# Three expert-row tiles a head turned ahead of the sweep, in halves over three buffer pairs, and zero writes moved behind the norm roots

## What is computed

```python
h = _rms(x, attn_norm_g[l])
proj = h @ w_in[l]                       # q, k, v (1024 each), then cb, cc, cx of the short convolution
q = _rms(q...); k = _rms(k...)           # per head norms, 8 heads
a = _diff_attention(q, k, v, lam)        # two softmaxes a head, their weighted difference, times v
a = (_rms(a, subln_g[l]) * (1.0 - lam_init)).reshape(b, s, ATTN_WIDTH)
c = _short_conv(cb, cc, cx, conv_w[l])
x = x + jnp.concatenate([a, c], axis=-1) @ w_out[l]
x = x + _peer(_rms(x, ffn_norm_g[l]), peer_w_q[l], peer_subkeys[l], peer_u[l], peer_v[l])
```

## Time and profile before

| what | value |
| --- | --- |
| median of 3 runs | 2966.29 us |
| the profiled execution | 2965.18 us, of which the span is 2963.4 us |
| PE, DVE, ACT, POOL busy | 98%, 80%, 35%, 51% of the span |
| granted TensorE clock | 0.995 over the span, 1.00 in the stretches shown below |
| HBM | 866.33 MB read, 112.33 MB written |

### The profile page before, as it was taken

The page is one execution under the profiler, slowest core; times in us unless marked ns, Lnnn a source line. Parts: engine busy times, 40 slices in busy tenths (PEclk is TensorE's granted clock), DMA queues, the critical chain, the costliest instruction groups (busy, mean ns, idle before and its releaser), DMA issues.

```text
span 2963.4 us, 40377 instructions
## 1 busy us (share of the span) xinstructions
PE 2892.9 (98%) x14993; PEld 2571.4 (87%) x14993; DVE 2356.5 (80%) x3050; ACT 1049.3 (35%) x1373; POOL 1510.2 (51%) x906
## 2 busy tenths in 40 slices
PE   8999999999999999999999999999999999999998
PEld 6888777888889999999999999999997788777777
DVE  6455677755688888988888898899777999998898
ACT  4122343341323333434333343334233333333333
POOL 1000232300016666665665666566867778877852
PEclk9999999999999999999999999999999999999999
DMA  8998777779658998999999899999999999999998
GB/s 297 332 348 278 253 237 252 226 289 332 225 187 305 320 340 302 337 320 330 309 322 337 305 339 316 333 343 356 338 348 395 412 415 410 417 418 419 419 417 357
DMA packets 324223, 980.65 MB, mean 331 GB/s; under 512 B 62756, under 2 KB 179504, under 8 KB 240752
## 3 DMA queue, kind: packets, MB, share of 16 engines
q1 hardware_dynamic: 179488, 508.60, 46.5%
q0 software_dynamic: 107008, 439.75, 41.3%
q10 hardware_dynamic: 37584, 30.43, 3.2%
HBM read 866.33 MB, written 112.33 MB: 330 GB/s over the span
## 4 chain that ended last, share of the span: by engine, by line
PE 66%; DVE 15%; DMA 10%; issue 4%; ACT 3%; POOL 1%; ACTq 0%; DVEq 0%; SPq 0%; POOLq 0%
PE ps L1827 21%; PE ps L1829 20%; PE ps L1828 20%; DMA v_two<-in_peer_v 9%; DVE x_rows L1685 3%; PE ps L2079 3%; DVE u_row L1676 2%; DVE v_lo L1725 2%; ACT v_hi L1196 2%; DVE x_one L1775 1%; DMA v_ring<-in_peer_v,experts 1%; DVE uT_lo L1670 1%; DVE uT_lo L1665 1%; PE ps L1910 1%; PE ps L1926 1%
## 5 line engine op out<-in xcount | busy, mean ns | idle before, releaser
L1827 PE MATMUL ps<-hT_hi,uT_hi 128*128 128x384 f32 x2048 | 699.0, 341 | 10.5 <-DVE uT_lo L1665 8.6
L1829 PE MATMUL ps<-h2T_lo,uT_hi 128*128 128x384 f32 x2048 | 686.1, 335 | 0.0
L1828 PE MATMUL ps<-hT_hi,uT_lo 128*128 128x384 f32 x2048 | 684.9, 334 | 0.0
L831 POOL DMA_INDIRECT gate_grid<-gates,grid_cells x256 | 541.5, 2115 | 107.4 <-issue 78.8
L1827 PE MATMUL ps<-v_hi,a_hi 128*128 128x512 f32 x1024 | 405.7, 396 | 31.5 <-DVE v_lo L1725 30.7
L1828 PE MATMUL ps<-v_hi,a_lo 128*128 128x512 f32 x1024 | 402.5, 393 | 0.0
L1829 PE MATMUL ps<-v_lo,a_hi 128*128 128x512 f32 x1024 | 402.3, 393 | 0.0
L1827 PEld LDWEIGHTS ps<-hT_hi,uT_hi 128*128 128x128 f32 x2048 | 384.7, 188 | 19.4 <-DVE uT_lo L1665 14.6
L1196 ACT ACTIVATE v_hi<-v_two 128x2048 fp32r<-128x2048 f32 x126 | 241.3, 1918 | 448.1 <-PE ps L1829 324.9
L1828 PEld LDWEIGHTS ps<-hT_hi,uT_lo 128*128 128x128 f32 x2048 | 385.0, 188 | 1.9
L1829 PEld LDWEIGHTS ps<-h2T_lo,uT_hi 128*128 128x128 f32 x2048 | 384.3, 188 | 0.0
(11 more groups left out here) (209 smaller groups left out, 4975.9 us busy)
## 6 DMA issues: line engine op xcount, KB each, us to landing
v_two<-in_peer_v SPq DMA_DIRECT2D x63, 2048.0 KB, 11.8
u_tile<-in_peer_u SPq DMA_DIRECT2D x72, 1024.0 KB, 8.0
u_tile<-uT_all SPq DMA_DIRECT2D x56, 1024.0 KB, 6.8
near_rows<-in_peer_u SPq DMA_DIRECT2D x40, 1024.0 KB, 8.3
uT_all<-near_turned SPq DMA_DIRECT2D x100, 256.0 KB, 7.0
w_raw<-in_w_in SPq DMA_DIRECT2D x24, 1024.0 KB, 9.3
wc_raw<-in_w_in SPq DMA_DIRECT2D x48, 512.0 KB, 6.6
far_rows<-in_peer_u SPq DMA_DIRECT2D x16, 1024.0 KB, 9.4
```

Source lines behind the costliest of these rows:

```text
L831: pool.indirect_dma_start(out=gate_grid, out_offset=bass.IndirectOffsetOnAxis(ap=grid_cells[:, d, col:col + 1], axis=0), in_=gates[:, 2 + ...
L1827: mm(out, a_hi, b_hi, start=first, stop=False)
L1828: mm(out, a_lo, b_hi, start=False, stop=False)
L1829: return mm(out, a_hi, b_lo, start=False, stop=last)
```

## The change

Seven more tiles, one for each of heads 0 to 6, are turned ahead: tile 6 of groups 0 to 6 of the sweep (`EXTRA_AT`). So three tiles a head are turned, in six halves (1024 of the 2048 columns, 512 KB each). Half i uses buffer pair (third, left, right)[i % 3]: left and right are the halves of the old pair, the third is new. DVE turns half 0 at the head's start, 1 and 2 where the first tile's halves were, 3 behind `combined(3)`, 4 and 5 behind `o_n`. SP loads the halves between the pieces, behind `wc_ready` of pieces 1 to 5. POOL stores each half by four DMAs of 128 KB in runs of 1 KB. The zeros move from the head's start to behind the two roots. Ahead of its loop over the heads SP now waits until the last q, k, v chunk is finished (the third pair lies where weights of that stage are), so pieces 2 and 3 of head 0 are issued behind that. In the sweep both u buffers can hold a turned tile. Some semaphores are merged.

```diff
 def turned_before(tile):
+    if tile % TOPK == EXTRA_AT:
+        return tile // TOPK < EXTRA
+    return tile % 2 == 1 and tile < 2 * ODD_TURNED
-    return tile % 2 == 1 and tile < 2 * TURNED
...
@@ SP @@
+            for t in range(TB):
+                sp.wait_ge(proj_done[t], QKV_CHUNKS)
             with sp.Fori(0, CT - 1) as j:
                 for p in range(PIECES):
                     sp.wait_ge(wc_ready, PIECES * j + p + 1)
                     conv_piece(j + (p + 2) // PIECES, (p + 2) % PIECES)
-                    if p in (2, 5):
-                        next_rows(NEAR, 2 * j + (NEAR_HEADS + p // 5))
+                    for i in ((), (0,), (1, 2), (3,), (4,), (5,))[p]:
+                        next_half(j, i)
...
+            sp.wait_ge(half_kept[THIRD], 16 * QUADS * HALF_USES)
             load_mix(MIX_ORDER[1])
@@ POOL @@
+            def store_half(x, row, half):
+                rows = uT_all[bass.ds(row * P, P), :].rearrange("(r d) (a h m) -> a h d r m", r=QUADS, a=QUADS, h=HALVES)
+                for a in range(QUADS):
+                    pool.dma_start(rows[a][half], half_turned[x][QUAD * a:QUAD * (a + 1), :, :, :].rearrange("d r k e -> d r (k e)"))\
+                        .then_inc(half_kept[x], 16)
...
             for j in range(HEADS):
-                for n in range(2 * j, 2 * j + 2):
-                    zero_cells(n)
                 if j > 0:
                     store_o(j - 1)
                 if j < HEADS - 1:
-                    keep_turned(NEAR_HEADS + 1 + 2 * j)
+                    for i in range(4):
+                        keep_half(j, i)
...
                 if j < HEADS - 1:
...
-                    keep_turned(NEAR_HEADS + 2 + 2 * j)
+                for n in range(2 * j, 2 * j + 2):
+                    zero_cells(n)
+                if j < HEADS - 1:
+                    for i in range(4, 6):
+                        keep_half(j, i)
...
@@ DVE @@
+            def turn_half_of_head(j, i):
+                x, use = half_of_head(i), 2 * j + i // 3
+                dve.wait_ge(half_in[x], 16 * (HALF_LOADS[x] + use) + 16)
+                dve.wait_ge(half_kept[x], 16 * QUADS * (HALF_STORES[x] + use))
+                turn_half(x)
...
                 if not last:
+                    turn_half_of_head(j, 3)
                     split_wc(j + 1, 1)
```

More of the change, by code:

```diff
@@ L454, in decoder_layer, with odd, odd_of_head, extra @@
         nc_block = ctx.enter_context(nc.Block())
[L457 to L462, removed]
+        def odd(pair, n):
+            k = n + pair * (NEAR_TURNED - EXTRA)
+            return 2 * k + 1, k
+        def odd_of_head(j, m):
+            k = NEAR_HEADS + 2 * j + m
+            return 2 * k + 1, k
+        def extra(j):
+            return TOPK * j + EXTRA_AT, ODD_TURNED + j
+        def store_turned(engine, pair, row, stored):
+            rows = uT_all[bass.ds(row * P, P), :].rearrange("(r d) (a m) -> a d r m", r=QUADS, a=QUADS)
             for a in range(QUADS):
@@ L465, in store_turned, with half_place, half_of_head, halves_turned @@
                     .then_inc(stored, 16)
+        def half_place(j, i):
+            place = extra(j) if i >= 4 else odd_of_head(j, 1 + i // 2)
+            return place, i % 2
+        def half_of_head(i):
+            return (THIRD, LEFT, RIGHT)[i % 3]
+        def halves_turned(j, i):
+            return 4 * (NEAR_HEADS + 1) + 2 * (6 * j + i)
         @nc_block.sync
@@ L475, in load_quarter, with load_rows, load_half, next_half @@
                     .then_inc(w_in_raw[q % 2], 16)
[L477 to L481, removed]
-                sp.wait_ge(seg_ready[pair], 4 * n + 4)
[L484 to L491, removed]
+            def load_rows(pair, tile):
+                sp.dma_start(seg_rows[pair][:, :], u_table[bass.ds(tile * P, P), :]).then_inc(seg_in[pair], 16)
+            def load_half(x, tile, half):
+                cols = slice(half * D // HALVES, (half + 1) * D // HALVES)
+                sp.dma_start(half_rows[x][:, :], u_table[bass.ds(tile * P, P), cols]).then_inc(half_in[x], 16)
+            def next_half(j, i):
+                (tile, _), half = half_place(j, i)
+                sp.wait_ge(seg_ready[NEAR], halves_turned(j, i) - 4)
+                load_half(half_of_head(i), tile, half)
+            def keep_turned(pair, n, place, then=None):
+                sp.wait_ge(seg_ready[pair], 4 * n + 4)
+                if then is not None:
+                    load_rows(pair, then[0])
+                store_turned(sp, pair, place[1], seg_stored[pair])
             def load_wi(c, q):
@@ L497, in load_qkv_weights, with keep_odd @@
             def load_qkv_weights():
+                def keep_odd(pair, n, last=False):
+                    keep_turned(pair, n, odd(pair, n), None if last else odd(pair, n + 1))
                 def chunk(c, first=False):
@@ L533, in far, with keep_odd @@
                     return FAR_QKV + 2 * c
+                def keep_odd(pair, n, last=False):
+                    seen = EXTRA if pair == NEAR else 0
+                    keep_turned(pair, n, odd(pair, n - seen), None if last else odd(pair, n - seen + 1))
                 for q in range(1, 4):
@@ L1412, in head @@
                                    vec[:, V_CONV:N_VEC].rearrange("p (a c) -> p a c", a=TAPS)[:, :, bass.ds(j, 1)]))
+                if not last:
+                    turn_half_of_head(j, 0)
                 def biased(qb):
@@ L1444, in head @@
                 if not last:
-                    turn_rows(NEAR, 2 * j + (NEAR_HEADS + 1), "heads", range(2))
+                    turn_half_of_head(j, 1)
                 split_wc(j, 4)
@@ L1449, in head @@
                 if not last:
-                    turn_rows(NEAR, 2 * j + (NEAR_HEADS + 1), "heads", range(2, 4))
+                    turn_half_of_head(j, 2)
                 biased(3)
@@ L1474, in head @@
                 if not last:
[L1475 removed]
+                    turn_half_of_head(j, 4)
+                    turn_half_of_head(j, 5)
                     norm_qk(j + 1, 1)
@@ L1519, in rest_of_chunk @@
                 split_wo(c + 1, 1)
-                turn_rows(NEAR, 3 * c + NEAR_OUT, "heads" if first else "out")
+                if first:
+                    for x in (LEFT, RIGHT):
+                        dve.wait_ge(half_kept[x], 16 * QUADS * (HALF_STORES[x] + HALF_USES))
+                turn_rows(NEAR, 3 * c + NEAR_OUT, "out")
             split_wo(0, 3)
```

172 lines of the change are left out of this document (104 added, 68 removed).

## The result

The changed kernel takes **3005.32 us** in the median of 4 runs (3003.94 to 3008.36), the kernel before 2966.32 (2965.81 to 2966.8); the ratio is 1.0137, with a 95% interval of 1.0125 to 1.0149. The forecast was 2962.2, its range 2956 to 2976. The profiled execution of the changed kernel is the one of 3008.36 us, with a span of 3006.6 and a granted clock of 0.985 over the span, where before had 0.995.

The account below looks back on a forecast made before the run. PE was taken to bound the heads and sweep groups 0 to 5, with group 6 nearly DVE's. Steps 1 to 5 summed as -10.5 + 2.2 + 0 + 4.2 + 0 = -4.1 us, giving 2962.2 us, range 2956 to 2976.

Parts of the forecast that it names:

- Step 1: Sweep: PE loses tile 6's transposes, 1.76 us a tile in groups 0 to 5, nothing counted in group 6; -10.5 us.
- Step 2: Start of the heads: SP's new wait delays pieces 2 and 3 of head 0, so PE stands once; +2.2 us.
- Step 3: DVE and POOL work in a head: extra half turns and store issues fit in free time, zeros delay none; 0 us.
- Step 4: DMA engines in a head: extra loads and stores leave transfers over, 0.6 us a head for seven heads; +4.2 us.
- Rival B: Heads: weight pieces starve in DMA queues, half 1 comes late, about 3 us a head; +12.7 us, 2979; chance 0.22.
- The rule weighed: DMA queues: each engine goes round its queues, taking a whole packet from one before changing; alone it would give rival B.
- Step 5: End of the heads: the last zeros, written later, delay following loads by up to 1 us within slack 1.8; 0 us.
- Rival A: Heads: left-over transfers are absorbed behind the sensitive piece, so step 4 is 0; -8.3 us, 2958.0; chance 0.37.
- Rival C: Sweep: DVE already sets the pace about tile 6, so the change doesn't shorten it; 2968 to 2975; chance 0.03.

Follow-up runs that it names:

- the kernel with the well-placed zeros: Changed kernel with a head's two zero DMAs parted, one behind the stores of half 2, one between the two roots: 2958.25 us, ratio 0.9971.
- the fastest kernel: Changed kernel with zero DMAs behind half 2's stores and between the roots, and SP's wait behind the issue of head 0's piece 3: 2953.47 us, ratio 0.9957.

## Why the prediction was wrong

**What bounds the kernel.** Right: PE bounded the heads without a wait, and they could only get longer.

**Step 1, right.** Forecast -10.5 in the sweep and nothing in group 6. From the first product of group 0 to that of group 6 it took 1036.4 us before and 1025.9 after; group 6 took 153.3 and 153.2. The whole time fell by 11.2 us in the run of that part alone. PE makes 1040 transposes instead of 1152.

**Step 2, the mechanism right, the size too small.** Forecast 2.2 us; the gap is 3.0 us (2.8 with that wait alone), inside the bounds of 1.9 to 4.8. What the sum lacked is that the wait costs more than its length: 4.7 us to the start of the sweep.

**Step 3, right as far as it goes.** PE waits for neither `o_ss` nor `qk_ss`, and with the zeros elsewhere DVE's 2.6 us more and POOL's 16 more issues cost nothing (heads of 40.90 us). Its last sentence, that the zeros behind the roots delay none, is true of the roots and says nothing of SP's loads.

**Step 4 is the one that failed.** Its amounts were good: with the zeros well placed the share is 0.93, and I had 0.91 to 0.97. But the sum spread the cost as bytes over free engine time and asked what was left at the end of the busy stretch. From that came 0.6 us a head, where 8.0 were measured. The sum had no term for the order in which POOL's and SP's transfers meet. I counted it as a gain that "the zeros now start just after the empty stretch"; just there SP issues piece 4. Before, that piece and the tile's load were issued 4.3 and 3.6 us ahead of the zeros (419.33 and 420.05 against 423.67). What the runs showed in its place is a wait for transfers that are issued behind the zeros: piece 4 lands 17 us and half 1 18.6 us after its issue, DVE stands for 8.55 us, PE for 5.2, and the slower clock comes on top. The bounds of 0 and 20 for seven heads did not hold the measured 48 either.

**Rival B, right in place and sign, too small in size.** I gave it 0.22 and 3 us a head. It took a piece's 13.0 us, the longest of the earlier trace rows, as the most that sharing could cost; 17 us were measured. But in the kernel before that 13.0 is itself a piece behind zeros. POOL's zeros and SP's next issues in head 3, and the landing of the first of these, piece 5:

```profile
423.67 1.78 POOL L776 DMA_DIRECT2D gate_grid<-zeros  x2
...
424.73 8.57 SPq L571 DMA_DIRECT2D wc_raw<-in_w_in  x2
...
DMA to landing us min/median/max: 12.9/12.9/12.9
```

In six heads there (342 to 588 us) piece 5 is issued 1.1 us behind the zeros and lands 11.4 to 13.0 us later; that costs PE nothing there. So the row did show a piece behind zeros. What it did not show is the rest of POOL's queue: there one store of 256 KB follows the zeros at once, here eight of 128 KB. With four of 256 KB behind them (the zeros' move alone) piece 4 took 15.1 us. This reading is argued from three kernels; no run varies the stores alone. Rival B also had no price for the clock. The argument against it, that DVE waited only 0.27 us today, was read under the old order and could not speak against the new one.

**The rule weighed.** I set it aside because the stores' rows had not agreed. In the changed kernel the two queues pass 1274 and 1743 packets in 20 us, fewer of POOL's than of SP's but more than twice the bytes. Cut finer, the queues from 391 to 394 and from 397 to 400 us:

```profile
q0 software_dynamic: 234, 0.89, 97.5%
...
q0 software_dynamic: 298, 0.81, 82.6%
q1 hardware_dynamic: 301, 0.15, 17.0%
```

From 397 to 400 us the queues pass nearly equal numbers. That agrees with the turn by packets of the Trainium skill ("DMA: Bandwidth & Descriptors", section "Queues, rings and completion order"), under which small packets that share with large ones get the smaller part of the bytes. From 391 to 394 us it does not: POOL's queue, with zeros in it, passes 234 packets and SP's none, though piece 4 was issued at 390.15. In the kernel with the zeros behind the stores, SP's queue passes 346 packets between 1.7 and 2.7 us after the issue of piece 4. So the load is late twice, by a start that comes some 3 us later and by the sharing behind it. Why it starts late stays open.

**Step 5, right, and rivals A and C.** Between 613 us and the first product no PE wait is added in the kernel with the well-placed zeros. Rival A's 2958.0 is what that kernel gives while SP's wait stands where the change has it (2958.25). Rival C falls with step 1.

**The books.** By the runs of one part each: -11.2 (sweep), +5 (SP's wait), +40 (zeros), together +34; measured +39. What is left lies in the heads: in the profiled executions six periods lose 48.0 us in the changed kernel and 39.1 with the zeros' move alone. So the third tile, which costs nothing where the zeros stand well, costs some 9 us where they stand badly. Which of its transfers does it was not parted.

## What to carry to other kernels

Before moving a large DMA, list what the other queues issue in the next 10 us or so and who waits for it; a transfer that nobody waits for does its harm to those that are issued behind it. Put it where the next urgent load has already been issued. A row in which some load stands behind such a transfer prices it only with what else stood in that queue; count what your order puts right behind it. Price a PE wait with the slower matmuls behind it.

## What the runs showed of the hardware

**A wait of PE costs more than its length.** PE's timeline behind the 5.20 us wait:

```profile
416.45 0.63 PE L1936 MATMUL ps<-hT_hi,wc_hi 128*128 128x512 f32 x1
416.88 0.63 PE L1937 MATMUL ps<-hT_hi,wc_lo 128*128 128x512 f32 x1
...
422.45 0.39 PE L1938 MATMUL ps<-hT_lo,wc_hi 128*128 128x512 f32 x1
422.68 0.40 PE L1936 MATMUL ps<-hT_hi,wc_hi 128*128 128x512 f32 x1
```

The step is 0.43 us at the 1.2 GHz level and 0.23 at 2.4. From the transposes at 414.43 to the first `apply_v` matmul behind them at 421.21 lie 6.78 us; the kernel before needs 3.64 for the same (438.25 to 441.89). So the slower clock adds 3.1 us to the 5.2 of the wait. In the kernel with one zero DMA moved two waits of 2.46 and 1.58 us made 6.9 (a head of 47.80). A single wait of 0.8 us, which the kernel before has too, left the clock at 1.00 (611 to 617 us).

**A DMA issue can hold the engine that makes it.** One issue of a half's load on SP took 9.25 us behind the zeros; in the fastest kernel the longest was 0.78 us. In this head it cost nothing by itself: it ended at 407.29, and SP's next piece had to wait until 411.9 for the split of piece 4 anyway (issued at 412.09).

**Where the same 2 MB of zeros a head stand** made anything from 2958 us (between the stores and between the roots) to 3005 us (behind the roots, ahead of piece 4), with 2967 only 4.5 us further on.
